# A gate stage with VectorE's later steps put two tiles on and some of its results kept in PSUM

## The reference, cut to what matters

```python
for i in range(DEPTH):
    h = rmsnorm(x, norm_pre[i])
    y = mixer_i(h)
    x = x + rmsnorm(y, norm_post[i])
    gate = jax.nn.sigmoid(rmsnorm(x, pe_norm[i]) @ pe_w_gate[i])
    x = x + gate * (p[i] @ pe_w_proj[i])
```

## Time and profile before

| | |
|---|---|
| median of 3 runs | 678.89 us (678.32 to 680.39) |
| profiled execution: its own time | 680.2 us |
| its span | 678.4 us |
| mean granted TensorE clock | 0.994 |
| TensorE busy | 638.2 us, 94% |
| VectorE busy | 414.5 us, 61% |
| ScalarE busy | 334.8 us, 49% |
| GpSimd busy | 313.3 us, 46% |

### The profile page before, as it was taken

One profiled execution on the slowest core, in us unless ns is written; L12 is line 12 of the kernel. 1 busy time (PEld: TensorE's weight loads), 2 busy tenths in 40 slices (PEclk: granted clock), 3 DMA queues, 4 the chain that ended last, 5 costly groups with the idle time before them and its releaser, 6 DMA issues.

```text
span 678.4 us, 9386 instructions
## 1 busy us (share of the span) xinstructions
PE 638.2 (94%) x2960; PEld 517.7 (76%) x2960; DVE 414.5 (61%) x801; ACT 334.8 (49%) x569; POOL 313.3 (46%) x412
## 2 busy tenths in 40 slices
PE   4979899999999999899988999999999999999897
PEld 1767787787878787688766778888888888887676
DVE  6657786867878687646686863424333343366864
ACT  7646575655655575455546553223231331455451
POOL 6465455656365455100176737564536643001771
PEclk9999999999999999899999999999999999999999
DMA  6234343333333343135001313332223232250032
GB/s 225 92 100 115 122 127 118 102 100 124 116 107 114 117 123 104 32 112 170 30 32 62 102 53 125 124 98 88 90 95 124 82 128 101 86 170 25 31 113 74
DMA packets 27161, 68.69 MB, mean 101 GB/s; under 512 B 3568, under 2 KB 10096, under 8 KB 27136
## 3 DMA queue, kind: packets, MB, share of 16 engines
q1 hardware_dynamic: 27136, 68.37, 30.9%
HBM read 66.23 MB, written 2.13 MB: 101 GB/s over the span
## 4 chain that ended last, share of the span: by engine, by line
PE 63%; DVE 16%; issue 9%; ACT 6%; POOL 3%; DMA 1%; DVEq 0%; SPq 0%; ACTq 0%; POOLq 0%
PE ps_pj L1062 18%; PE ps_pj L1064 18%; PE ps_pj L1063 18%; POOL w_lo L412 3%; DVE act_lo L954 2%; PE ps_tr L1071 2%; DVE k_st L871 2%; DVE xT L950 1%; ACT logit L523 1%; ACT k_st L569 1%; DVE logit L807 1%; DVE o_u L819 1%; DVE t_a L997 1%; PE ps_tr L1062 1%; DVE q_lo L863 1%
## 5 line engine op out<-in xcount | busy, mean ns | idle before, releaser
L412 POOL TENSOR_TENSOR w_lo<-w_raw,w_hi 128x256 fp32r<-128x256 f32 x324 | 256.1, 824 | 142.8 <-ACT w_hi L470 142.7
L1062 PE MATMUL ps_pj<-act_hi,w_hi 128*128 128x512 f32 (+1 forms) x744 | 297.5, 400 | 10.8 <-DVE act_lo L954 4.4
L1064 PE MATMUL ps_pj<-act_hi,w_lo 128*128 128x512 f32 (+1 forms) x744 | 290.1, 390 | 0.0
L1063 PE MATMUL ps_pj<-act_lo,w_hi 128*128 128x512 f32 (+1 forms) x744 | 289.4, 389 | 0.0
L1062 PEld LDWEIGHTS ps_pj<-act_hi,w_hi 128*128 128x128 f32 x744 | 140.7, 189 | 44.0 <-issue 9.6
L1064 PEld LDWEIGHTS ps_pj<-act_hi,w_lo 128*128 128x128 f32 x744 | 140.2, 189 | 29.7
L1063 PEld LDWEIGHTS ps_pj<-act_lo,w_hi 128*128 128x128 f32 x744 | 140.8, 189 | 24.7
L470 ACT CAST w_hi<-w_raw 128x1024 fp32r<-128x1024 f32 x96 | 100.0, 1049 | 80.3 <-DMA w_raw<-in_weights 67.5
L445 POOL TENSOR_TENSOR acc<-acc,sq 128x512 f32<-128x512 f32 x14 | 21.3, 1524 | 123.0 <-ACT sq L615 122.1
L420 POOL TENSOR_TENSOR bias<-bias,future 128x128 f32<-128x128 f32 x64 | 34.3, 568 | 80.5 <-DMA bias<-negc_scratch 80.5
L523 ACT ACTIVATE logit<-logit,nmax 128x128 f32<-128x128 f32 (+1 forms) x64 | 36.2, 565 | 60.1 <-DVE nmax L798 59.9
(11 more groups left out here) (141 smaller groups left out, 778.4 us busy)
## 6 DMA issues: line engine op xcount, KB each, us to landing
w_raw<-in_weights SPq DMA_DIRECT2D x100, 512.0 KB, 3.4
bias<-negc_scratch SPq DMA_DIRECT2D x16, 256.0 KB, 7.3
bias<-negc_scratch SPq DMA_DIRECT2D x16, 192.0 KB, 6.2
xT<-in_xT SPq DMA_DIRECT2D x8, 256.0 KB, 5.9
bias<-negc_scratch SPq DMA_DIRECT2D x16, 128.0 KB, 4.8
out<-xT SPq DMA_DIRECT2D x7, 256.0 KB, 2.0
bias<-negc_scratch SPq DMA_DIRECT2D x16, 64.0 KB, 3.4
p_in<-in_pT SPq DMA_DIRECT2D x2, 512.0 KB, 4.5
```

Of the source, the lines that this page charges most:

```text
L412: last = nc.gpsimd.tensor_tensor(w_lo[place % RING][:, tiles], w_raw[stream(place) % RAW][:, tiles], w_hi[place % RING][:, tiles], ALU.sub ...
L1062: nc.tensor.matmul(out, w_h, a[0][:, k, tokens], start=k == first, stop=False)
L1063: nc.tensor.matmul(out, w_h, a[1][:, k, tokens], start=False, stop=False)
L1064: end = nc.tensor.matmul(out, w_l, a[0][:, k, tokens], start=False, stop=k == last)
```

## The change

- VectorE's `gate_rest` (act_lo and the added square) is done for tile m - 2 and stands ahead of the wait for the tanh of tile m; it stood behind the steps of tile m, for tile m - 1. Two calls follow the last tile.
- For tiles 4 to 7 the gated embedding `(t_b + 1) * ple` is written over `ple` in its PSUM bank and read from there; it went to `t_a`.
- Norm 3's sum is kept in `ps_wide` and no longer in `acc`: ScalarE's first square is written there, after VectorE has scaled tile 2 (which empties the bank), VectorE adds into it, and both parts are taken from it.
- Norms 2 and 5 (`GATE_NORMS`): VectorE goes on when TensorE has made `ps_o` and scales tiles 0 and 1 from it. ScalarE's copy to `rs` is put after the first tanh, behind both scalings; the scaling of tile 2 waits for it. The conversion of slot 4 now follows the root directly, ahead of that copy.

```diff
--- before.py
+++ after.py
@@ -66,6 +66,8 @@
 
 TR_BANKS = 3
 POST_NORMS = [1, 4]
+GATE_NORMS = [2, 5]
+SUM_IN_PSUM = 3
 USE_V = 0
 USE_T = -8
 
@@ -297,6 +299,10 @@
 
             return n - sum(post < n for post in POST_NORMS)
 
+        def sums(n):
+
+            return ps_wide[:] if n == SUM_IN_PSUM else acc[:]
+
         def last_step(slot):
 
             for l in range(2):
@@ -496,7 +502,7 @@
                 else:
                     act.wait_ge(acc_done, KT * n)
                 wait(act, st_done, n)
-                nc.scalar.copy(acc_hi[:], acc[:]).then_inc(acc_hi_done, 1)
+                nc.scalar.copy(acc_hi[:], sums(n)).then_inc(acc_hi_done, 1)
 
             def norm_root(n):
 
@@ -605,7 +611,12 @@
             turn(PAIRS, 0, False, True)
 
             def square(n, src):
-                if n % KT == 0:
+                if n == 2 * KT:
+
+                    act.wait_ge(acc_ready, n // KT + 1)
+                    act.wait_ge(g_scaled, WIDE + 1)
+                    nc.scalar.activation(ps_wide[:], src, ACT.Square).then_inc(acc_done, 1)
+                elif n % KT == 0:
 
                     act.wait_ge(acc_ready, n // KT + 1)
                     nc.scalar.activation(acc[:], src, ACT.Square).then_inc(acc_done, 1)
@@ -674,7 +685,6 @@
                 gate_copy(0)
                 gate_copy(1)
                 norm_root(3 * l + 2)
-                norm_spread(3 * l + 2)
                 gate_weight(4)
                 def gate_next(m):
 
@@ -686,6 +696,8 @@
 
                 for m in range(KT):
                     if m == 1:
+                        act.wait_ge(g_scaled, (WIDE + 1) * l + 2)
+                        norm_spread(3 * l + 2)
                         gate_weight(m + 4)
 
                     for i, tokens in enumerate(parts(l, m)):
@@ -721,7 +733,7 @@
         def _(dve):
             def norm(n, meanwhile=None):
                 dve.wait_ge(acc_hi_done, n + 1)
-                nc.vector.tensor_tensor(acc_lo[:], acc[:], acc_hi[:], ALU.subtract).then_inc(acc_ready, 1)
+                nc.vector.tensor_tensor(acc_lo[:], sums(n), acc_hi[:], ALU.subtract).then_inc(acc_ready, 1)
                 if meanwhile:
                     meanwhile()
                 dve.wait_ge(root_done, n + 1)
@@ -731,7 +743,7 @@
                 wait(dve, spread_done, n)
                 nc.vector.tensor_copy(r_row[:], r_tok[:].rearrange("p (t o) -> p t o", o=1).to_broadcast([P, TT, P])
                                       ).then_inc(r_row_done, 1)
-                if n in POST_NORMS:
+                if n in POST_NORMS + GATE_NORMS:
                     dve.wait_ge(spread_done, n + 1)
                 else:
                     dve.wait_ge(rs_ready, rows_copied(n + 1))
@@ -908,7 +920,8 @@
 
                     dve.wait_ge(sq_ready, n - n // KT)
                     dve.wait_ge(acc_done, n)
-                    nc.vector.tensor_tensor(acc[:], acc[:], sq[n % 2][:], ALU.add).then_inc(acc_done, 1)
+                    total = sums(n // KT + 1)
+                    nc.vector.tensor_tensor(total, total, sq[n % 2][:], ALU.add).then_inc(acc_done, 1)
 
             def chain(ins):
 
@@ -973,8 +986,9 @@
                     if m < WIDE:
                         s = STEP_GATE[l] + m
                         dve.wait_ge(pj_free[s % 2], s // 2 + 1)
-                        nc.vector.tensor_tensor(t_a[m][:], g_raw[m][:], rs[:], ALU.mult).then_inc(g_scaled, 1)
+                        nc.vector.tensor_tensor(t_a[m][:], g_raw[m][:], ps_o[:], ALU.mult).then_inc(g_scaled, 1)
                     elif m == WIDE:
+                        dve.wait_ge(rs_ready, rows_copied(3 * l + 3))
                         dve.wait_ge(wide_done, 2 * l + 2)
                         nc.vector.tensor_tensor(t_a[m % 2][:], ps_wide[:], rs[:], ALU.mult).then_inc(g_scaled, 1)
                     else:
@@ -991,15 +1005,17 @@
                     elif m > 1:
                         gate_scale(m)
 
+                    gate_rest(m - 2)
                     ple = pleT[:, m, :] if m < PLE_STEPS else ps_ple[m - PLE_STEPS][:]
+                    gated = t_a[m % 2] if m < PLE_STEPS else ps_ple[m - PLE_STEPS]
                     for i, tokens in enumerate(parts(l, m)):
                         dve.wait_ge(g_tanh, KT * l + m + i + 1)
-                        link = chain(nc.vector.scalar_tensor_tensor(t_a[m % 2][:, tokens], t_b[m % 2][:, tokens], 1.0,
+                        link = chain(nc.vector.scalar_tensor_tensor(gated[:, tokens], t_b[m % 2][:, tokens], 1.0,
                                                                     ple[:, tokens], ALU.add, ALU.mult))
                         dve.wait_ge(v_self, link)
-                        nc.vector.scalar_tensor_tensor(xT[:, m, tokens], t_a[m % 2][:, tokens], 0.5, xT[:, m, tokens],
+                        nc.vector.scalar_tensor_tensor(xT[:, m, tokens], gated[:, tokens], 0.5, xT[:, m, tokens],
                                                        ALU.mult, ALU.add).then_inc(x_new, 1)
-                    gate_rest(m - 1)
+                gate_rest(KT - 2)
                 gate_rest(KT - 1)
                 if l == 1:
                     continue
```

## The result

The changed kernel takes 672.02 us (median of 4 runs, 670.55 to 673.59) against 678.72 us for the kernel before (4 runs): a ratio of 0.990, interval 0.9881 to 0.9919. That is 6.7 us; 6.1 were forecast, and 672.8 us.

The account below looks back on a forecast made before the run. TensorE, busy 94% of the span, was taken as the bound, so only its gate-stage gaps could be gained: 5.0 us in layer 0 plus 1.1 in layer 1, 6.1 off the 678.89 us median, giving 672.8, range 671.6 to 676.0.

Parts of the forecast that it names:

- The bound: Both gate stages: TensorE's gaps cap the gain at 6.5 us; VectorE is late behind gaps put down to "issue".
- The start: Start of layer 0's gate stage: first tanh at 359.1 against 361.02, scaling of tile 3 ends 3.7 us earlier.
- The steady state and the end: Layer 0's gate stage: VectorE needs 3.3 to 3.8 us per tile against TensorE's 5.44; end margin 0.1 us.
- 5.0 + 1.1 us: Gains forecast for the gate stages: 5.0 us in layer 0 and 1.1 us in layer 1.
- The 0.1 that I had left before tile 5: Layer 0's gate stage: TensorE still loses about 0.1 us before tile 5, in place of 3.04.
- PSUM writes: VectorE instructions writing PSUM in the gate stages: taken at 0.69 us, between bounds of 0.68 and 1.23.
- rivals 1 and 2: Gate stages: VectorE partly late, gain 2.1 to 4.9, chance 0.18; or PSUM instructions costing more, 3 us slower, chance 0.05.
- All off TensorE's path except at the end: Gate stage: PSUM results take up to 0.54 us per tile from VectorE, on TensorE's path only at the end.
- The wait on the square: Layer 0's gate stage: tile 0's square waits for tile 2's scaling; tile 2's tanh 0.6 us later, act_lo fills 0.8.
- Rival 3: Gate stages at TensorE's pace expose the weight slots; nearly all is given back, 677 to 679 us, chance 0.09.

## Why the prediction was right

**The bound.** TensorE's gaps as the ceiling, and VectorE's lateness behind those put down to "issue": right. The order put back reopens the gap before tile 5 and nothing else.

**The start.** Forecast: slot 4 converted at once, the table loaded ahead of the wait, first tanh 2.5 us behind the root, scaling of tile 3 ended 11.5 behind. Measured: 2.43 and 11.21. What I did not see is that the earlier w_lo collides with the scalings and that ps_o is what avoids it. In the sum it cost nothing, since the change has both; as a reason it was incomplete.

**The steady state and the end.** No gap but the one before the second convolution product (0.36 us in slots, forecast 0.3). TensorE asks for acc_lo 35.91 us behind the root (forecast 36.2), and the margin is 0.26 us, not 0.1. The prediction's own terms left nothing at all: VectorE's queue ended at 392.9 and TensorE asked at 392.8. That the margin is small is shown: 0.66 to 0.78 us come back when adds and steps are slowed.

**The term that was mis-sized.** 5.0 + 1.1 us were forecast, 5.39 + 1.32 measured. A gap costs more than its idle time. TensorE behind the gap at 371.90, the kernel before:

```profile
372.20 0.40 PE L1063 MATMUL ps_pj<-act_lo,w_hi 128*128 128x512 f32 x1
```

The second matmul starts 0.30 us after the first, not 0.227; behind w_lo it is 363.62 - 363.28 = 0.34, and a few more come at 0.23 to 0.24. So the 24 matmuls of a tile behind a gap take 5.56 to 5.58 us instead of 5.44. For the three gaps of layer 0 that go this is 0.39 us, a term that the prediction put at nothing. With it the stage closes: 5.37 of gaps, less 0.36 for the one that stays, plus 0.39, is 5.40 against the 5.39 measured. The 0.1 that I had left before tile 5 did not appear. In layer 1 the two gaps of 1.14 us bring some 0.2 of the same kind. The total, 672.8 against 672.02, is closer than this could promise: single runs of the changed kernel lie between 670.55 and 673.59.

**PSUM writes.** I took 0.69 us between bounds of 0.68 and 1.23; they take 0.68 to 0.70, and the table load ran ahead of its wait, so rivals 1 and 2 had nothing to stand on. The Trainium skill ("VectorE: DVE Perf Modes", "The TRN2 errata") gives an instruction that reads PSUM 62 cycles more than one that reads SBUF. The trace does not show them, nor anything of the kind for writes: adds in PSUM take 685 to 693 ns. "All off TensorE's path except at the end" holds for the changed kernel only: in the old order the slowed steps lie on the path, and the embedding alone gains 1.08 us.

**The wait on the square.** Costed at nothing, with act_lo of tile 0 named as its cover. With the new order that is so: 362.88 follows 361.52 + 1.32 without idle. With that cover gone (the sum in PSUM, old order) it costs 0.53 to 0.58 us of TensorE's gap in three pairs of kernels (3.41 against 2.88, 3.46 against 2.88, 1.92 against 1.35), and in the first two half clock stood behind it.

**Rival 3** did not come: no w_lo is waited for in the changed kernel. GpSimd's pieces went from 998 to 739 ns at the median, which I had not counted.

## What to carry to other kernels

Before moving work off a late engine's path, look at what its earlier or later place sets off on the engine beside it: here one operand in PSUM kept an instruction at 0.69 us where its twin took 1.2, and two weight conversions moved to where ScalarE idles were worth a gap each. A wait in an in-order queue costs nothing only while what stands behind it has cover, so price it in the order in which it will run. Cut the span at events that both kernels share before explaining a difference: 2.9 of the 9.6 us here had nothing to do with the change.

## What was not expected of the hardware

- Behind a gap of 3.41 and of 3.46 us TensorE's granted clock was 0.50 and 0.51 of full over 3 us, the lower of its two levels (1.2 GHz), worth 1.6 us; behind 2.88 us (two executions) it stayed full. Elsewhere in the kernel it fell to 0.50 behind gaps of 1.16 to 1.51 us in three of fourteen executions, and not in the others, so no length of gap seen here decides it.
- VectorE writes PSUM, and reads and writes the same bank in one instruction, as fast as SBUF: 678 to 697 ns for 128x512 fp32 (the same kernel's adds in SBUF, outside the gate stages, take 683 to 693). ScalarE's one square into PSUM took 0.60 us, against 0.62 into SBUF.
- An instruction with two SBUF operands goes from 0.69 to 1.23 us beside GpSimd's w_lo, and GpSimd's pieces from 0.73 to 1.2; with one operand in PSUM neither pays. The Trainium skill says as much ("SBUF — State Buffer", "Who interferes with whom"): two SBUF inputs on VectorE contend with a GpSimd instruction that reads SBUF, one does not; the trace agrees.
